# Attention of a two-block model on one NeuronCore: exponentials and weights each a slot behind the scores, high and low queries stacked, compressed branch last

## The reference

```python
qn = rmsnorm(heads(nq, NSA_HEADS), nsa_qnorm_g[i])
q_nope = qn.reshape(B, KVH, G, T, dh)
q_rope = partial_rope(qn, cos, sin).reshape(B, KVH, G, T, dh)
kc = rmsnorm(compress(heads(kcm, KVH), ...), nsa_knorm_g[i, 0])
vc = compress(heads(vcm, KVH), ...)
s_cmp = jnp.einsum('bgntd,bgcd->bgntc', q_nope, kc) * scale
p_cmp = masked_softmax(s_cmp, cmp_mask)
o_cmp = jnp.einsum('bgntc,bgcd->bgntd', p_cmp.astype(vc.dtype), vc)
...
k_sl = partial_rope(rmsnorm(heads(ksl, KVH), nsa_knorm_g[i, 1]), cos, sin)
o_slc = selected_attn(q_rope, k_sl, heads(vsl, KVH), sel, scale)
k_wn = partial_rope(rmsnorm(heads(kwn, KVH), nsa_knorm_g[i, 2]), cos, sin)
o_win = window_attn(q_rope, k_wn, heads(vwn, KVH), scale)
gates = jax.nn.sigmoid(ngate).reshape(B, T, 3, KVH, G).transpose(2, 0, 3, 4, 1)[..., None]
o_nsa = gates[0] * o_cmp + gates[1] * o_slc + gates[2] * o_win
y_nsa = o_nsa * jax.nn.silu(nz)
h = h + jnp.concatenate([y_hg, y_nsa], axis=-1) @ w_out[i]
```

## Time and profile before

| what | value |
|---|---|
| median of 3 runs | 3296.68 us (3296.47 to 3296.89) |
| the profiled execution: its own time | 3290.16 us |
| the profiled execution: span from first to last instruction | 3288.4 us |
| PE / PEld busy | 2964.8 us (90%) / 2435.8 us (74%) |
| DVE / ACT / POOL busy | 1373.0 us (42%) / 835.1 us (25%) / 1913.9 us (58%) |
| mean granted TensorE clock | 0.938 of full speed |
| one layer's attention, 376.30 to 551.84 us | 175.54 us |

### The profile page before, as it was taken

One profiled execution on the slowest core, in us unless ns is written; L12 is line 12 of the kernel. 1 busy time (PEld: TensorE's weight loads), 2 busy tenths in 40 slices (PEclk: granted clock), 3 DMA queues, 4 the chain that ended last, 5 costly groups with the idle time before them and its releaser, 6 DMA issues.

```text
span 3288.4 us, 40055 instructions
## 1 busy us (share of the span) xinstructions
PE 2964.8 (90%) x14036; PEld 2435.8 (74%) x14036; DVE 1373.0 (42%) x2052; ACT 835.1 (25%) x1726; POOL 1913.9 (58%) x889
## 2 busy tenths in 40 slices
PE   5887888988887898999999899999989999899998
PEld 4777656877775577877878688887877878688786
DVE  3766455357655534455423222121455423322021
ACT  2332333333324324113222222021113222222021
POOL 4634302574361045746869467786846869468785
PEclk9989679999895899989999999999989999999999
DMA  5212100231120012312333123332312333123232
GB/s 116 77 34 65 45 1 20 77 88 52 47 77 13 1 52 80 96 52 78 96 97 116 58 78 100 92 96 86 104 52 84 92 95 118 56 84 97 90 97 76
DMA packets 280370, 241.16 MB, mean 73 GB/s; under 512 B 42272, under 2 KB 212320, under 8 KB 280160
## 3 DMA queue, kind: packets, MB, share of 16 engines
q1 hardware_dynamic: 270240, 235.28, 24.5%
q10 hardware_dynamic: 9920, 3.18, 0.5%
HBM read 236.32 MB, written 2.10 MB: 73 GB/s over the span
## 4 chain that ended last, share of the span: by engine, by line
PE 75%; DVE 13%; issue 6%; ACT 5%; SPq 0%; POOL 0%; DVEq 0%; DMA 0%; ACTq 0%; POOLq 0%
PE bank L1698 9%; PE bank L1701 9%; PE bank L1702 9%; PE bank L1656 7%; PE bank L1660 7%; PE bank L1659 7%; PE bank L726 3%; PE bank L729 3%; PE bank L730 3%; PE bank L1628 2%; PE bank L966 2%; PE bank L834 1%; PE bank L980 1%; PE bank L778 1%; PE bank L708 1%
## 5 line engine op out<-in xcount | busy, mean ns | idle before, releaser
L2434 POOL TENSOR_TENSOR whi<-raw,zero 128x1024 fp32r<-128x1024 f32 (+2 forms) x440 | 830.6, 1888 | 1290.3 <-PE bank L726 619.3
L2436 POOL TENSOR_TENSOR wlo<-raw,whi 128x1024 fp32r<-128x1024 f32 (+2 forms) x440 | 1075.9, 2445 | 34.6
L1656 PE MATMUL bank<-xhi,whi 128*128 128x512 f32 x928 | 364.8, 393 | 0.0
L1659 PE MATMUL bank<-xlo,whi 128*128 128x512 f32 x928 | 363.0, 391 | 0.0
L1660 PE MATMUL bank<-xhi,wlo 128*128 128x512 f32 x928 | 362.9, 391 | 0.0
L1698 PE MATMUL bank<-whi,xhi 128*128 128x512 f32 x832 | 329.9, 397 | 11.3 <-DVE xlo L2062 7.6
L1701 PE MATMUL bank<-wlo,xhi 128*128 128x512 f32 x832 | 327.3, 393 | 0.0
L1702 PE MATMUL bank<-whi,xlo 128*128 128x512 f32 x832 | 327.2, 393 | 0.0
L726 PE MATMUL bank<-whi,xhi 128*128 128x512 f32 (+2 forms) x640 | 239.7, 375 | 12.8 <-ACT v L1061 12.8
L729 PE MATMUL bank<-wlo,xhi 128*128 128x512 f32 (+2 forms) x640 | 235.1, 367 | 0.0
L730 PE MATMUL bank<-whi,xlo 128*128 128x512 f32 (+2 forms) x640 | 234.1, 366 | 0.0
(11 more groups left out here) (435 smaller groups left out, 5279.9 us busy)
## 6 DMA issues: line engine op xcount, KB each, us to landing
raw<-in_w_in SPq DMA_DIRECT2D x144, 512.0 KB, 3.6
raw<-in_w SPq DMA_DIRECT2D x132, 512.0 KB, 3.8
raw<-in_w_pg SPq DMA_DIRECT2D x16, 512.0 KB, 3.8
raw<-in_w_o SPq DMA_DIRECT2D x16, 512.0 KB, 3.8
raw<-in_xa_k SPq DMA_DIRECT2D x16, 512.0 KB, 3.9
raw<-in_xa_q SPq DMA_DIRECT2D x16, 512.0 KB, 4.0
raw<-in_xa_v SPq DMA_DIRECT2D x16, 512.0 KB, 3.8
raw<-in_xa_o SPq DMA_DIRECT2D x16, 512.0 KB, 3.8
```

Source lines behind the costliest of these rows:

```text
L1656: mm = pe.matmul(o, wh, rhs[0][:, k, :], start=(k == 0), stop=False)
L1659: pe.matmul(o, wh, rhs[1][:, k, :], start=False, stop=False)
L2434: nc.gpsimd.tensor_tensor(whi[:, s, 0:n], raw[:, s, 0:n], zero[:, :].to_broadcast([P, n]), ALU.add).then_inc(hi_split, 1)
L2436: nc.gpsimd.tensor_tensor(wlo[:, s, 0:n], raw[:, s, 0:n], whi[:, s, 0:n].bitcast(F32), ALU.subtract).then_inc(lo_split, 1)
```

## The change

Each row of scores goes through four steps in place of two. `score` is now PE and DVE alone; `exp` is ACT's part; `recip` takes the reciprocals of one row's sums; `weigh` scales one row, with the gate and the reciprocal as the two scalars of one DVE instruction. A slot is laid out as: turn, exponentials of the rows scored in the slot before, reciprocals of the rows exponentiated in the slot before, one or two new scores, weights of the rows just reciprocated, one step of the compressed branch, the value product of two turns earlier. There are 46 slots in a layer (40 of them with a turn). Ten rows rotate (the two new ones in `vv`, free once POOL has split it).

The scores are made of stacked operands: `qhl` holds the high part of a head's queries in one half of the partitions and the low part in the other, `khh` the high part of the keys in both halves, `kll` the low part in both. Two passes of 128 partitions take the place of three of 64 (and low·low is now included). ACT and DVE write the halves with copies of 64 partitions: 8 ACT and 8 DVE instructions for the queries (before 4 and 4) and 8 and 8 for the keys (before 2 and 2).

`c_val` now closes the output bank rather than opens it. The turning of the keys leaves `k_norm` and becomes `k_turn`, just ahead of `q_rope`; the rotation of the queries becomes `q_rot`, ahead of `hg_turn`; `p_turn` moves behind the attention, since `pT` and `kll` share memory. The other lines of the diff are names of signals and tables.

```diff
@@ attention_steps
-    for t, (u, kt) in enumerate(TURNS):
+    while t < len(TURNS):
+        if not out:
+            compressed = [("c_score", 0), ("c_exp", 0), ("c_weigh", 0), ("c_turn", 0)]
+        slot = []
+        u, kt = TURNS[t]
         qt, g, br = UNITS[u]
...
+        turned = all(i in weighed for i in rows_of(u))
+        if turned:
+            slot += [("turn", t)]
+            t += 1
+            if qt and kt == 0 and (g, br) == (0, 0):
+                compressed = [(kind, qt) for kind in ("c_score", "c_exp", "c_weigh", "c_turn")]
+        slot += [("exp", i) for i in scored]
+        weigh, shared, scored = shared, scored, []
+        slot += [("recip", i) for i in weigh]
+        for _ in range(2):
+            if j < len(ROWS) and (j < P_ROWS or t > TURNS.index((ROWS[j - P_ROWS][0], UNITS[ROWS[j - P_ROWS][0]][0]))):
+                v, i = ROWS[j]
+                if scored and (UNITS[v][0], i) != (2, 3):
+                    break
+                slot += [("score", j)]
+                scored += [j]
+                j += 1
+        slot += [("weigh", i) for i in weigh]
+        weighed |= set(weigh)
+        slot += compressed[:1]
+        compressed = compressed[1:]
+        if turned and t > TURN_LEAD:
+            slot += product(t - 1 - TURN_LEAD)
+        out += slot
@@ steps_one
-    s += nz[:1] + [("q_norm",)] + nz[1:2] + [("k_norm",), ("c_in", 0)] + nz[2:3] + hid[0] + [("c_in", 1)] + nz[3:] + hid[1]
+    s += nz[:1] + [("q_norm",)] + nz[1:2] + [("k_norm",), ("c_in", 0)] + nz[2:3] + hid[0] + [("c_in", 1)] + nz[3:] + hid[1] + [("q_rot",)]
...
-    s += [("c_out",), ("q_rope",), ("nz_gate", 0), ("nz_gate", 1), ("c_key",), ("p_turn",), ("nz_gate", 2), ("nz_gate", 3)]
+    s += [("c_out",), ("k_turn",), ("q_rope",), ("nz_gate", 0), ("nz_gate", 1), ("c_key",), ("nz_gate", 2), ("nz_gate", 3)]
...
-    s += main + out0[:1] + last[0] + last[1] + out0[1:] + tm("out1", "w_out", 512, 512)
+    s += main + [("p_turn",)] + out0[:1] + last[0] + last[1] + out0[1:] + tm("out1", "w_out", 512, 512)
@@ tensor_one, step_score
-                    for a, b in ((0, 0), (0, 1), (1, 0)):
-                        pe.matmul(G.ps(name)[:, w * n:(w + 1) * n], qTr[part, a, i * heads + w, qt * P:(qt + 1) * P],
-                                  kTn[part, b, br, 0:n], start=(w == 0 and a == b), stop=False)
+                    a = qhl[:, g * NG + i * heads + w, qt * P:(qt + 1) * P]
+                    pe.matmul(G.ps(name)[:, w * n:(w + 1) * n], a, khh[:, g, br, 0:n], start=(w == 0), stop=False)
+                    pe.matmul(G.ps(name)[:, w * n:(w + 1) * n], a, kll[:, g, br, 0:n], start=False, stop=False)
@@ scalar_one
+            def step_k_turn(step):
                 for br in range(2):
-                    hi(kTn[:, 0, br, :], ("kT", br))
-
+                    act.wait_ge(*G.filled(("kT", br), l))
+                    for g, part in enumerate(GROUP):
+                        nc.scalar.copy(khh[GROUP[1 - g], g, br, :], G.ps(("kT", br))[part, :])
+                        nc.scalar.copy(khh[part, g, br, :], G.ps(("kT", br))[part, :]).then_inc(*sigs["hi"].up())
@@ vector_one
+            def step_recip(step):
+                j = step[1]
+                u, i = ROWS[j]
+                heads = HEADS[UNITS[u][0]]
+                dve.wait_ge(*G.evacuated(("s", j), l))
+                nc.vector.reciprocal(coef[:, u % 8, i * heads:(i + 1) * heads], sums[:, u % 8, i * heads:(i + 1) * heads]).then_inc(*cf_ready.up())
...
-                for m in range(NG):
-                    ins = ts(p_share(u, m), p_share(u, m), coef[:, u % 8, m:m + 1], None, ALU.mult)
+                dve.wait_ge(*cf_ready.at(l, j + 1))
+                for m in range(i * HEADS[qt], (i + 1) * HEADS[qt]):
+                    hh = g * NG + m
+                    ins = ts(p_share(u, m), p_share(u, m), gts[:, qt, 1 + br, hh:hh + 1], coef[:, u % 8, m:m + 1], ALU.mult, ALU.mult)
```

More of the change, by code:

```diff
@@ L201 @@
 TURNS = [(u, kt) for u, (qt, _, _) in enumerate(UNITS) for kt in range(qt + 1)]
-P_ROWS, TURN_SLOTS, TURN_LEAD = 8, 3, 2
-CLOSES = [UNITS[u][2] == 1 and kt == UNITS[u][0] for u, kt in TURNS]
+P_ROWS, TURN_SLOTS, TURN_LEAD = 10, 3, 2
 def rows_of(u):
@@ L210, in attention_steps @@
 def attention_steps():
-    out, j, turned = [("c_score", 0)], 0, 0
+    out, t, j, scored, shared, compressed = [], 0, 0, [], [], []
     def product(t):
@@ L217, in product @@
         qt, g, br = UNITS[u]
[L218 to L243 removed]
+        after = [("c_val", qt, g), ("y_part", qt, g)] if br == 1 and kt == qt else []
@@ L327, in groups_one @@
         return [(("t", step[1]), (7, 0, 1))]
-    if kind == "c_val":
-        return [(("o_a", *step[1:]), (2, 3))]
+    if kind == "value" and TURNS[step[1]][1] == 0 and UNITS[TURNS[step[1]][0]][2] == 0:
+        return [(("o_a", *UNITS[TURNS[step[1]][0]][0:2]), (2, 3))]
     return []
@@ L951, in step_c_val @@
                 name = ("o_a", qt, g)
-                pe.wait_ge(*G.free(name, l))
                 pe.wait_ge(*G.evacuated(("cp", qt, g), l))
-                pe.matmul(G.ps(name)[:, :], vc[0:NCMP].rearrange("p g d -> p (g d)"), pcT[0:NCMP, g, :], start=True, stop=False)
+                pe.matmul(G.ps(name)[:, :], vc[0:NCMP].rearrange("p g d -> p (g d)"), pcT[0:NCMP, g, :], start=False, stop=True)\
+                    .then_inc(*G.full(name))
             def step_score(step):
@@ L1195, in step_q_rope @@
                 for n in range(NG):
-                    hi(qTr[:, 0, n, :], ("qr", n))
+                    act.wait_ge(*G.filled(("qr", n), l))
+                    for g, part in enumerate(GROUP):
+                        nc.scalar.copy(qhl[part, g * NG + n, :], G.ps(("qr", n))[part, :]).then_inc(*sigs["hi"].up())
             def step_k_norm(step):
```

110 lines of the change are left out of this document (53 added, 57 removed).

## The result

The changed kernel takes 3222.4 us (3221.1 to 3223.9), the kernel before 3296.6 us: a ratio of 0.978 (0.976 to 0.980). The forecast was 3218 us. It came out within 5 us because larger errors ran against each other, and most of what follows is about those.

A forecast was written before the change was run, and what follows sets the result against it. No engine was full; one chain of scores, weights, turn and value bound the attention. VectorE's 504.7 us plus 7.7 for the half clock gave 512.4, saving 39.4 us in each of two layers: 3218 us, range 3198 to 3254.

The forecast's parts named there:

- The sum: Layer one: VectorE's time to 504.7 us plus 7.7 for TensorE's half clock; attention ends at 512.4, 39.4 earlier.
- Up to the first maximum: From the keys' turn leaving `k_norm` to the first maximum: taken at 379.3 where it was 382.75, 3.4 us gained.
- the half copies: ScalarE's 16 copies of 64 partitions for keys and queries: .62 us each with the gap, 10.0 us in all.
- First maximum to last value product: The attention of layer one: VectorE's work of 102.3 us plus issue time, waits and TensorE's half clock; 131.4 us.
- The 97.15 us: VectorE's work over the four query tiles before the change, the base to which the forecast added up to 102.3 us.
- first turns: First turn of each of 16 units: VectorE idle for 1.12 us at each, 17.9 us in all.
- Behind the last value product: End of attention: last value product .7 us, then `p_turn` 1.0 (2.7 if the output product waits for its copies).
- The clock: TensorE's granted clock in the attention: half in tile 0, rising in tile 1, near full from tile 2; +7.7 us.
- The fourth rival: TensorE stays at 1.2 GHz throughout the attention: 9.0 us a layer slower than before, 3315 us; chance .04.
- The third: Rival: VectorE waits for the high part in every slot, 27 us a layer more, 3272 us; chance .08.
- The first: Rival: clock stays low through tile 1 and in part of tiles 2 and 3, 3236 to 3253 us; chance .17.
- second: Rival: everything in the attention at the full clock and issue time free, 49.1 us gained a layer, 3198 us; chance .08.

The follow-up runs named there:

- the third pass: The changed kernel with a third pass of 128 partitions (the low keys' pass made twice) in each row of scores: 3224.0 us.
- the four changes: The changed kernel with `p_turn` later, weights ahead of the maximum, `q_rot` earlier and GpSimd's split of the values held back, all together: 3208.7 us.

## Why the prediction came out, step by step

The sum put the output product of layer one at 512.4; it starts at 516.29. The error of 3.9 us is made of three:

- **Up to the first maximum: 379.3 forecast, 386.27 measured, +7.0.** This part was wrong in sign: 3.4 us earlier was forecast, 3.5 later came. `c_in` was to start 2.6 us earlier and started .3 later (+2.9): GpSimd's split moved up with TensorE's product and stretched the keys' rotation. From there to the end of the root the sum had 34.8 us, and it was 38.3 (+3.6). The sum let .7 of the gain be lost there. It charged nothing for `q_rot` in the place it is moved *to*, ahead of `hg_turn` on VectorE, which cost 2.2 us: the move was priced where the step left, not where it arrived. And it took TensorE's time in the hidden layer as unchanged, where the first half ran at .50 and not .71, 2.1 us net. From root to first maximum 18.5 was forecast and 19.0 came (+.5): the half copies took 9.6 us on ScalarE for the 10.0 of the sum (.60 each, the whole of the bound, and .70 on VectorE), and the gates 9.3 for 8.5 beside GpSimd's split.
- **First maximum to last value product: 131.4 forecast, 126.3 measured, -5.1.** The tiles took 27.5, 28.0, 35.4 and 35.3 where 26, 30, 37 and 39 stood. VectorE was busy for 94.6 us, not 102.3. The mechanism was right, and the term was mis-sized. The 97.15 us is right as a busy time, but what was added to it was durations, and those overlap where operations stand back to back: the slot shown under the experiments takes 1.77 us (471.17 to 472.94), where its durations sum to 2.05. Counted from start to start, the 44 reciprocals took 3.4 us where 7.3 stood, and low parts and maxima fell from 52.0 to 47.7 us where no change stood. The weights grew by 5.2 us and not 3.8, though the second scalar adds .06 to each duration, as taken. Two gates, 1.3 us of the 97.15, lay ahead of the first maximum and were counted there too. VectorE's idle time was 31.7 us, with 29.1 forecast: 13 of the 16 first turns waited, for 1.57 us on average where 1.12 stood, and 8 turns inside units, which the sum had covered, waited too.
- **Behind the last value product: 1.7 forecast, 3.8 measured, +2.1.** `p_turn`'s own time was right (1.09), but its banks were called not needed at once, and they were the output product's. The bound of 2.7 for that case was given and not taken.

The clock came as forecast, near half in tile 0 (.60) and full from tile 2 on (1.00, .95), .91 in tile 1. What it did in tile 0 did not: the sum had TensorE's 26.7 us of work at the half clock set the pace there, but TensorE was busy for 18.5 of the 27.5 us. The tile's time was right by waits, of VectorE for the high part and of TensorE for weights. By the rule of the Trainium skill on transposes that the forecast weighed (TensorE: Matmul & The Clock Gate, Part 4: PE-mode transpose), slots with a turn in each might have kept it low; tile 2 holds twelve turns, 48 transposes, and ran at 1.00, so the trace doesn't agree. Nor does a stretch of the kernel before, in which TensorE did nothing but transposes from 365.56 to 368.60, at .50, and had 1.00 from 368.70 on. The fourth rival, TensorE at the half clock throughout, is out by tile 2's row too. The third, VectorE waiting in every slot, is out too: 21 waits for 40 turns. The first and second were not what happened. (The price of the first is added up wrong: 5.4 + 6.7 + 4 is 16.1 us a layer and not 17.4, so 3250 us and not 3253.)

That the forecast of 3218 us lies within 5 us of 3222.4 is largely luck: +7.0 and +2.1 against -5.1 in layer one. Even so the profiled execution came out 9.7 us above its sum (3221.1 for 3211.4): 3.9 of layer one, 5.3 of layer two, which gained 34.1 us and not 39.4, and .6 at the end. And the sum then added 6.5 us for the distance from the profiled execution to the median, which was 1.3 this time; that took 5.2 us off the error.

## What to carry to other kernels

Where no engine is full, look at the order before the work: with the same VectorE work to .2 us, laying each consumer a slot behind its producer took half of its idle time away, while a TensorE pass added to every score cost 3 to 6.5 us a layer. When a step moves, price it in the queue that it enters, with what stands behind it there, and look up what a part that gets earlier will start on the other engines: here a GpSimd split that stretched two-input VectorE operations, and an idle time that moved to where TensorE then ran at half its clock. Size a stretch by the distance between starts of operations that stand back to back, not by their durations.

## What was not expected of the hardware

The distance from layer to layer takes only a few values over fourteen kernels: 590.50, 590.50 and 590.52, then 593.92 to 593.94 in four, 597.32 to 597.34 in three, 600.69, 631.47 and 634.89, steps of about 3.4 us, with one in between (600.30, the third pass). Single changes that gained 3.3 to 4.1 us in their own stretches all moved it by 3.41, and one that gained 1.5 us in its own, `q_rot` earlier, by nothing. What is missing turns up between the output product and the next layer's keys' rotation: that stretch takes 404.1 to 406.8 us in the thirteen changed kernels, though only the late `p_turn` edits anything in it. That is a part of why the four changes didn't add up. What sets the steps was not tested; the granted clock is a candidate, no more. For work on this kernel it means that a saving under 3 us a layer may show as nothing, or as 3.4.
